# Hybrid retention and attention block on one core: GpSimd's sums for the first projection units, the last gates and the first tokens' keys placed elsewhere

## The reference, cut to what matters

```python
rq, rk, rv, rg, fq, fk, fv, ff = jnp.split(proj, points, axis=-1)
ret = retention(rotary(heads(rq, RET_HEADS), pos),
                rotary(heads(rk, RET_HEADS), pos) * (RET_DK ** -0.5),
                heads(rv, RET_HEADS))[:, PAD:]
ret = head_norm(ret).reshape(b, l, RET_HEADS * RET_DV) * jax.nn.silu(rg)
fox = forgetting_attention(heads(fq, FOX_HEADS), heads(fk, FOX_HEADS), heads(fv, FOX_HEADS), pad(logf))[:, PAD:]
mixed = jnp.concatenate([ret, fox], axis=-1).astype(h.dtype)
```

## Time and profile before

| | |
|---|---|
| three runs | 2966.33, 2971.05, 2980.05 us |
| median | 2971.05 us |
| profiled execution, own time | 2969.91 us |
| its span | 2968.1 us |
| last retention head and pair projection in the span | about 526 to 863 us |

### The profile page before, as it was taken

One profiled execution on the slowest core, in us unless ns is written; L12 is line 12 of the kernel. 1 busy time (PEld: TensorE's weight loads), 2 busy tenths in 40 slices (PEclk: granted clock), 3 DMA queues, 4 the chain that ended last, 5 costly groups with the idle time before them and its releaser, 6 DMA issues.

```text
span 2968.1 us, 40210 instructions
## 1 busy us (share of the span) xinstructions
PE 2885.6 (97%) x14600; PEld 2089.5 (70%) x14600; DVE 1444.0 (49%) x4030; ACT 630.8 (21%) x1285; POOL 1272.9 (43%) x1140
## 2 busy tenths in 40 slices
PE   8999999999999999998999999999999999999998
PEld 4478888888875555554555767787777777777765
DVE  6665656565246767663677532333333333332326
ACT  2222111210025555452111101011111111111114
POOL 3443434366730110101345334555555555555645
PEclk9999999999999999999999999999999999999999
DMA  6500010111120103005444457888898899999996
GB/s 221 177 6 13 18 44 1 29 29 29 31 71 7 55 10 115 12 7 192 150 144 159 128 189 226 249 276 268 262 273 269 267 289 279 307 303 302 316 260 249
DMA packets 181015, 462.08 MB, mean 156 GB/s; under 512 B 26072, under 2 KB 98600, under 8 KB 155080
## 3 DMA queue, kind: packets, MB, share of 16 engines
q1 hardware_dynamic: 133872, 339.23, 32.4%
q0 software_dynamic: 44640, 111.84, 15.9%
q10 hardware_dynamic: 2304, 8.39, 0.7%
HBM read 345.44 MB, written 113.92 MB: 155 GB/s over the span
## 4 chain that ended last, share of the span: by engine, by line
PE 52%; DVE 1%; issue 1%; POOL 0%; ACT 0%
PE ps L2861 24%; PE ps L2802 12%; PE ps L2661 8%; PE ps L2717 3%; PE ps L2799 2%; PE ps L2727 1%; PE ps L2680 1%; PE ps L2750 0%; PE ps L2671 0%; POOL moe_fin L2456 0%; PE ps L2648 0%; PE ps L2701 0%; DVE moe_xT L2018 0%; PE ps L2690 0%; DVE moe_fin L2106 0%
## 5 line engine op out<-in xcount | busy, mean ns | idle before, releaser
L2374 POOL DMA_INDIRECT moe_xg<-t_rows,index x433 | 417.9, 965 | 173.7 <-issue 141.5
L2861 PEld LDWEIGHTS ps<-moe_xT,moe_wg 128*128 128x128 f32 x2048 | 353.0, 196 | 48.1 <-issue 34.3
L2861 PE MATMUL ps<-moe_xT,moe_wg 128*128 128x192 f32 (+22 forms) x2048 | 379.6, 338 | 3.3 <-issue 3.1
L2861 PE MATMUL ps<-moe_xT,moe_wu 128*128 128x192 f32 (+22 forms) x2048 | 376.1, 337 | 0.0
L2861 PEld LDWEIGHTS ps<-moe_xT,moe_wu 128*128 128x128 f32 x2048 | 354.1, 196 | 4.8
L2802 PE MATMUL ps<-moe_wd,moe_hh 128*128 128x512 f32 (+12 forms) x800 | 353.9, 592 | 0.0
L1918 DVE TENSOR_TENSOR moe_hh<-moe_sl,ps 128x256 f32<-128x256 f32 (+19 forms) x144 | 53.6, 372 | 561.8 <-ACT moe_sl L2515 329.6
L2395 POOL DMA_INDIRECT base_rows<-moe_yo,index x100 | 165.0, 1650 | 371.6 <-DVE moe_yo L2032 282.3
L2802 PEld LDWEIGHTS ps<-moe_wd,moe_hh 128*128 128x128 f32 (+12 forms) x800 | 142.3, 180 | 169.1 <-issue 168.8
L2018 DVE STREAM_TRANSPOSE moe_xT<-moe_xg 128x256 f32<-128x256 f32 x433 | 235.3, 609 | 47.2 <-DMA moe_xg<-t_rows,index 41.2
L1253 POOL TENSOR_TENSOR fox_diag<-fox_c,fox_causal 128x128 f32<-128x128 f32 x128 | 55.9, 458 | 449.7 <-DVE fox_mx L1282 444.9
(11 more groups left out here) (352 smaller groups left out, 4652.4 us busy)
## 6 DMA issues: line engine op xcount, KB each, us to landing
moe_wg<-in_we_gate SPq DMA_DIRECT2D x64, 1024.0 KB
moe_wu<-in_we_up SPq DMA_DIRECT2D x64, 1024.0 KB
moe_wd<-in_we_down SPq DMA_DIRECT2D x64, 1024.0 KB
fox_c<-ck SPq DMA_DIRECT2D x8, 1032.0 KB, 8.9
emb_xin<-in_x SPq DMA_DIRECT2D x16, 512.0 KB, 3.9
h_rows<-emb_hr SPq DMA_DIRECT2D x16, 512.0 KB, 2.8
ret_w<-in_w_in SPq DMA_DIRECT2D x16, 512.0 KB, 6.6
moe_yt<-h_rows SPq DMA_DIRECT2D x16, 512.0 KB
```

The source lines that it names most:

```text
L2374: pool.indirect_dma_start(out=xg[g % NXG][:, :], out_offset=None, in_=quarters, in_offset=bass.IndirectOffsetOnAxis(ap=route.index4[:, AT4 ...
L2861: ins = pe.matmul(out, w[:, c, f:FF:FC], xT[u][:, c, 0:n], start=(c == 0), stop=(c == DC - 1))
```

## The change

Three things are moved, and one of them takes fewer matmuls.

*Sums for the first units.* The four token sums of fox unit 0 are no longer made behind the last retention round, but one each in the last head's rounds j = 2 to 5, behind the round's own token sums. Pair 0's weight sums, four in round 5 before, are made in rounds 6 and 7, two each. Unit 1's token sums wait for the first product of the fox projection instead of the last one of the retention.

*Last gates.* The eight gate pairs of the last head stood four each in units 1 and 2, behind the adds of `SIXTH`, `SEVENTH`, `FIFTH` and `FOURTH`. They stand two each in units 1 to 4 now, behind `SEVENTH` and `FOURTH`.

*First tokens' keys.* For pairs 1 to 3 they are multiplied behind unit i = 1 of the pair before, with the key weights not changed yet: eight matmuls. For that TensorE waits for the pair's key weights to have landed, and part 1 of the weight sums waits for the keys. A list `ORDER` counts the products.

```diff
@@ -267,7 +267,6 @@
 
 
 FOX_UNITS = SEQ // BANK
-FOX_PRODUCTS = 1 + PRODUCTS * FOX_UNITS
 
 
 def fox_weight_sums(eng, ahead, p, part):
@@ -280,6 +279,8 @@
         eng.tensor_tensor(s1[:, :, :], wk[:, 0:k, :], wk[:, k:DC, :], ALU.add).then_inc(made, 1)
     if part == 1:
         eng.wait_ge(made, 4 * p + 1)
+        if p >= 1:
+            eng.wait_ge(ahead.fox_proj, ahead.fox_meta_done(p))
         eng.tensor_tensor(wk[:, 0:k, :], wk[:, 0:k, :], wq[:, 0:k, :], ALU.subtract).then_inc(made, 1)
     if part == 2:
         eng.wait_ge(made, 4 * p + 1)
@@ -289,18 +290,22 @@
         eng.tensor_tensor(s4[:, :, :], wq[:, k:DC, :], s2[:, :, :], ALU.subtract).then_inc(made, 1)
 
 
-def fox_token_sums(eng, ahead, hT, g):
+def fox_token_sum(eng, ahead, hT, g, part):
 
     k, s, made = DC // 2, ahead.ftok[g], ahead.fox_tsum
     t0 = META + BANK * (g % FOX_UNITS)
     t1, t2 = t0 + 2 * P, t0 + 4 * P
     b11, b12, b21, b22 = hT[:, 0:k, t0:t1], hT[:, 0:k, t1:t2], hT[:, k:DC, t0:t1], hT[:, k:DC, t1:t2]
-    eng.tensor_tensor(s[:, 0, :, :], b12, b11, ALU.subtract).then_inc(made, 1)
-    eng.tensor_tensor(s[:, 2, :, :], b12, b22, ALU.subtract).then_inc(made, 1)
-    eng.wait_ge(made, 4 * g + 1)
-    eng.tensor_tensor(s[:, 1, :, :], b22, s[:, 0, :, :], ALU.subtract).then_inc(made, 1)
-    eng.wait_ge(made, 4 * g + 3)
-    eng.tensor_tensor(s[:, 3, :, :], b21, s[:, 1, :, :], ALU.subtract).then_inc(made, 1)
+    if part == 0:
+        eng.tensor_tensor(s[:, 0, :, :], b12, b11, ALU.subtract).then_inc(made, 1)
+    if part == 1:
+        eng.tensor_tensor(s[:, 2, :, :], b12, b22, ALU.subtract).then_inc(made, 1)
+    if part == 2:
+        eng.wait_ge(made, 4 * g + 1)
+        eng.tensor_tensor(s[:, 1, :, :], b22, s[:, 0, :, :], ALU.subtract).then_inc(made, 1)
+    if part == 3:
+        eng.wait_ge(made, 4 * g + 3)
+        eng.tensor_tensor(s[:, 3, :, :], b21, s[:, 1, :, :], ALU.subtract).then_inc(made, 1)
 
 
 def flat(ap):
@@ -761,12 +766,14 @@
                 if j in (4, 5) and h + 1 < RH:
                     weight_sums(pool, ahead, h + 1, 2 * (j - 4))
                     weight_sums(pool, ahead, h + 1, 2 * (j - 4) + 1)
-                if j == 5 and h == RH - 1:
-                    for part in range(4):
-                        fox_weight_sums(pool, ahead, 0, part)
-            fox_token_sums(pool, ahead, hT, 0)
-            pool.wait_ge(proj, RH * HEAD_PRODUCTS)
-            fox_token_sums(pool, ahead, hT, 1)
+                if 2 <= j < 6 and h == RH - 1:
+                    fox_token_sum(pool, ahead, hT, 0, j - 2)
+                if j >= 6 and h == RH - 1:
+                    fox_weight_sums(pool, ahead, 0, 2 * j - 12)
+                    fox_weight_sums(pool, ahead, 0, 2 * j - 11)
+            pool.wait_ge(ahead.fox_proj, 1)
+            for part in range(4):
+                fox_token_sum(pool, ahead, hT, 1, part)
             norm(RH - 1)
 
         @block.scalar
@@ -1118,15 +1125,28 @@
         step0 = [sum(steps[:n]) for n in range(NT + 1)]
         FUNITS = [(p, i) for p in range(PAIRS) for i in range(FOX_UNITS)]
 
+        ORDER = []
+        for g, (p, i) in enumerate(FUNITS):
+            ORDER += [(g, which) for which in range(PRODUCTS)]
+            if g == 0:
+                ORDER.append(("meta", 0))
+            if i == 1 and p + 1 < PAIRS:
+                ORDER.append(("meta", p + 1))
+        COUNT = {what: n + 1 for n, what in enumerate(ORDER)}
+
         def done(g, product):
 
-            p, i = FUNITS[g]
-            return FOX_PRODUCTS * p + PRODUCTS * i + (i > 0) + product + 1
+            return COUNT[g, product]
 
         def meta_done(p):
 
-            return FOX_PRODUCTS * p + PRODUCTS + 1
-
+            return COUNT["meta", p]
+
+        def pair_done(p):
+
+            return COUNT[FOX_UNITS * (p + 1) - 1, THIRD]
+
+        ahead.fox_meta_done = meta_done
         ADDS = {SIXTH: 1, SECOND: 2, SEVENTH: 3, FIFTH: 5, FOURTH: 6, THIRD: 7}
         RING = (0, 1, 3, 2, 4, 5, 6, 7)
         groups = [[list(range(s, min(s + 2, z))) for s in range(0, z, 2)] for z in steps]
@@ -1209,20 +1229,20 @@
                 for b in range(2):
                     sp.dma_start(ahead.mix[b][:, :], mixed[P * b:P * (b + 1), :]).then_inc(ahead.mix_in[b], 16)
 
-            sp.wait_ge(proj, FOX_PRODUCTS)
+            sp.wait_ge(proj, pair_done(0))
             sp.wait_ge(ahead.fox_wsum, 4 * 2)
             weights(2)
-            sp.wait_ge(proj, 2 * FOX_PRODUCTS)
+            sp.wait_ge(proj, pair_done(1))
             sp.wait_ge(ahead.fox_wsum, 4 * 3)
             weights(3)
-            sp.wait_ge(proj, 3 * FOX_PRODUCTS)
+            sp.wait_ge(proj, pair_done(2))
             sp.wait_ge(added, PRODUCTS * 3 * FOX_UNITS)
             pair_gates(0)
             sp.wait_ge(proj, done(len(FUNITS) - 2, THIRD))
             sp.dma_start(causal[:, :], square[:, SQ_CAUSAL:SQ_CAUSAL + P]).then_inc(tab, 16)
             pair_values(0)
             pair_values(1)
-            sp.wait_ge(proj, PAIRS * FOX_PRODUCTS)
+            sp.wait_ge(proj, len(ORDER))
             pair_gates(1)
             for n, (p, t) in enumerate(order):
                 if n == 2 * TILES + 1:
@@ -1238,7 +1258,8 @@
             for g in range(2, len(FUNITS)):
                 if g >= 3:
                     pool.wait_ge(proj, done(g - 2, THIRD))
-                fox_token_sums(pool, ahead, hT, g)
+                for part in range(4):
+                    fox_token_sum(pool, ahead, hT, g, part)
             pool.memset(onesf[:, :], 1.0).then_inc(ones_set, 1)
             pool.wait_ge(tab, 16)
             for n, (p, t) in enumerate(order):
@@ -1333,19 +1354,18 @@
                 n0, t0, t1 = PRODUCTS * g, BANK * i, META + BANK * i
                 *p1, u2, u3, u4 = ahead.fadd[p]
                 p1 = p1[g % 2]
-                gate = lambda x: ahead.gate_pair(dve, RH - 1, x + 4 * (g - 1)) if g in (1, 2) else None
+                gate = lambda x: ahead.gate_pair(dve, RH - 1, x + 2 * (g - 1)) if 1 <= g < 5 else None
                 dve.wait_ge(first_c, g + 1)
                 dve.wait_ge(proj, done(g, SIXTH))
                 if g >= 1:
                     dve.wait_ge(added, n0 - PRODUCTS + 5)
                 add(g, SIXTH, u2[:, :], p1[:, :])
-                gate(0)
                 dve.wait_ge(proj, done(g, SECOND))
                 add(g, SECOND, qT[p][:, t0:t0 + 2 * P], p1[:, :])
                 dve.wait_ge(proj, done(g, SEVENTH))
                 dve.wait_ge(added, n0 + 1)
                 add(g, SEVENTH, u3[:, :], u2[:, :])
-                gate(1)
+                gate(0)
                 dve.wait_ge(proj, done(g, FIFTH))
                 if g >= 1:
                     dve.wait_ge(added, n0)
@@ -1354,10 +1374,9 @@
                 if g == 0:
                     dve.wait_ge(*ahead.mix_out[0])
                 add(g, FIFTH, kT[p][:, t1 + 2 * P:t1 + 4 * P], u3[:, :])
-                gate(2)
                 dve.wait_ge(proj, done(g, FOURTH))
                 add(g, FOURTH, kT[p][:, t1:t1 + 2 * P], u3[:, :])
-                gate(3)
+                gate(1)
                 if i >= 2 and p + 1 < PAIRS:
                     for part in (2 * i - 4, 2 * i - 3):
                         fox_weight_sums(dve, ahead, p + 1, part)
@@ -1368,7 +1387,7 @@
             dve.wait_ge(*ahead.ret_att)
             for g in range(len(FUNITS)):
                 project(g)
-            dve.wait_ge(proj, PAIRS * FOX_PRODUCTS)
+            dve.wait_ge(proj, len(ORDER))
             dve.wait_ge(*ahead.mix_out[1])
             for u in range(len(units[0])):
                 bias(0, u)
@@ -1433,9 +1452,9 @@
                 if g >= 2:
                     act.wait_ge(added, PRODUCTS * (g - 2) + 2)
                 nc.scalar.copy(ahead.fadd[p][g % 2][:, :], ps[:, RING[(done(g, FIRST) - 1) % len(RING)], 0:2 * P]).then_inc(first_c, 1)
-                if i == 0:
-                    act.wait_ge(proj, meta_done(p))
-                    nc.scalar.copy(kT[p][:, 0:META], ps[:, RING[(meta_done(p) - 1) % len(RING)], 0:META]).then_inc(meta_c, 1)
+                for m in [x for x in range(PAIRS) if x == 0 == g or x >= 1 and g == FOX_UNITS * (x - 1) + 1]:
+                    act.wait_ge(proj, meta_done(m))
+                    nc.scalar.copy(kT[m][:, 0:META], ps[:, RING[(meta_done(m) - 1) % len(RING)], 0:META]).then_inc(meta_c, 1)
                 if i == 2 and p + 1 < PAIRS:
                     act.wait_ge(w_s[0], 16 * (p + 2))
                     wq = flat(ahead.wqks[p + 1][0][:, :, :])
@@ -1469,16 +1488,13 @@
                     pe.wait_ge(*ahead.v_copied)
                 old = count - len(RING)
                 if old >= 1:
-                    p, x = divmod(old - 1, FOX_PRODUCTS)
-                    if x == PRODUCTS:
-                        pe.wait_ge(meta_c, p + 1)
+                    g, product = ORDER[old - 1]
+                    if g == "meta":
+                        pe.wait_ge(meta_c, product + 1)
+                    elif product == FIRST:
```

(20 more changed lines are left out.)

## The result

| | before | changed |
|---|---|---|
| median, measured side by side | 2966.55 us (2964.69 to 2980.05) | 2954.43 us (2953.49 to 2958.96) |
| profiled execution | 2969.91 us, span 2968.1 | 2953.49 us, span 2951.7 |
| ratio | | 0.995, interval 0.9931 to 0.9968 |

On another chip the same pair stood at 2969.48 and 2959.69 us (0.997, 0.9959 to 0.9981).

A forecast was written before the change was run, and what follows sets the result against it. TensorE, busy for 97% of the span, was taken as the bound. Keys 2.7 + last head 4.2 - gates 0.5 = 6.4 us off 2969.91 gave 2963.5, with 1.1 for the median 2964.6 us; range 2956 to 2974.

The forecast's parts named there:

- Last head: Last retention head's steps: 5.0 us of lost time go, 0.8 comes back behind round j = 2; 4.2 us off.
- Keys: First tokens' keys in pairs 1 to 3: four of twelve matmuls fewer each, 2.7 us off on TensorE's path.
- Gates: Projection units 2 to 4: weight sums still caught by GpSimd, TensorE's stall and slow clock 6.2 for 5.7, 0.5 us lost.
- rival B: Second gate's L665 in unit 3 misses its window: 2.3 us more, 2967, or 2970 if caught singly; chance 0.15.
- Store: Head 3's store delays pair 2's weights in SP's queue; they land at 22, wanted at 24.2: hidden by 2 us.
- Rival E: Norm's small power also blocks the last head's rotations at j = 2: 1.2 us more, 2966; chance 0.08.
- rival C: Rotations pushed over the next round in all six rounds with an extra GpSimd operation: slower, 2976 us; chance 0.07.
- A shift before the attention passes on to the end one for one, since TensorE is the bound behind it as well.: Step of the sum: the whole 6.4 us gained before the attention reaches the end of the execution.
- So such a wait brings no slow clock: In rival A: after 2.28 us of idle in the last head the next turn lasts 0.38 as all do.
- Cost nothing: Later start of unit 1's token sums: they end at 11 and are wanted at 16.5, so no cost.
- Zero cost: Moved keys' new VectorE wait before the in-place difference: covered by six products (10 us), so no cost.
- the half per cent: 15 us, about what a measurement can tell from no change; chances: faster 0.10, slower 0.04, the same 0.86.

The follow-up runs named there:

- the kernel with the one line put back: Kernel before with the moved sums alone, but unit 1's sums again wait for the last retention product; 2966.32 against 2969.93 us for before (0.9989).

## Why the prediction was right, and where it was wrong

In the last head and the projection the mechanism came as described. *Last head*: one rotation caught behind j = 2, one in the next step, TensorE idle for 0.79 us for 0.8 forecast (1.0 on the step); heads 4.1 us shorter where the clock episodes are alike (472.25 and 468.11), for 4.2. *Keys*: sixteen records in pairs 1 to 3, no wait at them. *Gates*: the wait before `SIXTH` of unit 4 is 4.3 us in three of four executions, for 4.4, with the slow clock behind it, by the forecast way, but for L666 in place of L670 being caught in the first gate. In the fourth it is 6.54, 2.2 more, for which rival B had 2.3; the prediction's margins there are 0.1 us, so that the profile of the result fell on the forecast's side is luck in part. *Store*: hidden; once the wait of 4.3 was gone, and with gates caught, so that the last was done 15.0 us behind unit 4's start for the 12 forecast, 1.7 us of it came into view; the cover was about as thin as forecast. Rival E is refuted by the 0.28 beside the power, rival C by even steps.

Wrong was the size, 6.4 us forecast and 12.1 measured. These steps failed:

1. *"A shift before the attention passes on to the end one for one, since TensorE is the bound behind it as well."* It doesn't. With twelve matmuls fewer, one of the two waits for issue in the shared experts goes: 1.8 us net, a term that the prediction put at nothing and that is in none of its rivals.
2. *"So such a wait brings no slow clock"*, read from one turn of 0.38 behind 2.28 us of idle. With the old last head the step behind it lasted 10.5 us in 4 of 7 executions and 8.8 in the others, so removing the wait was worth 5.0 and about half of 1.7 more: an estimate of 0.9 us from these counts.
3. *The unchanged heads were taken as constant.* Their clock episodes differ by up to 3.4 us between executions, and the two profiles of the result had the two ends. This is in the 16.4 us between the profiled executions; in a median it averages out.
4. *The base.* The median of three, 2971.05, was 4.5 above that of six executions beside the changed kernel: 2966.55 less 6.4 is 2960.2. Of the 10.2 us between the forecast 2964.6 and the measured 2954.43 these are 4.5, and the size of the gain is the other 5.7.

Steps 1 and 2 are 2.7 of the 5.7; the cause of the other 3 is open. Where they lie can be said. Over three executions of before and four of the changed kernel, on more than one chip, the heads are 5.6 shorter, the projection 2.7 (forecast 2.2), the shared experts to the end 1.9, and the rest, which no part of the change reaches, 3.9; 14.1 in all. Of the rest, 1.5 us lie between the scores and the output projection (511.0 before, 509.5 changed). Other kernels, with and without each part, show both values and some between, and what sets it is open.

Two more steps were wrong but cost nothing in the whole. The start of unit 1's sums: "Cost nothing" looked only at when TensorE wants the sums; they also push GpSimd into VectorE's gates, 3.6 us with the sums alone. The prediction's walk began at unit 2 and did not see it. In the whole only two gate pairs stand in unit 1, one of them was caught, and VectorE had idle time again before unit 2:

```profile
665.21 2.16 DVE L666 TENSOR_SCALAR ret_ret<-ret_ret,ret_mv,ret_rstd 128x128 f32<-128x128 f32 x2
...
675.34 0.42 DVE L1350 TENSOR_TENSOR fox_u2e<-ps,fox_p10e 128x256 f32<-128x256 f32 x1 [4.87 <-PE ps L1521]
```

The keys: "Zero cost" left out that 1.8 us of keys ahead of unit 2 give VectorE its window back, 4.3 us of gain with the keys alone. The walk through units 2 and 3 of the whole contained these 1.8 us, so its 4.4 us came out right. By the half per cent, "the same" and "faster" are hard to part here: the interval reaches from 3.2 to 6.9 thousandths.

## What to carry to other kernels

Two engines that exclude each other at a port are one resource with two queues: judge a moved operation by whom it meets there, not only by who waits for its result, and put the one that feeds the bound engine first in each free window. Parts of a change that meet in one window must be walked through together; alone, these gave 0.9 and 9.3 us of gain and 7.0 of loss, together 9.8. A wait seen once in a profile has a price with a spread, and so has a stretch that nobody changed; read several executions before taking either as fixed.

## What the runs showed of the hardware

**Waits for issue.** DMA packets of the kind instruction run all through the execution, and each of the 26 waits of TensorE for issue in the shared experts, 0.7 to 4.3 us long, ends 2.2 to 3.7 us after the start of such a packet. That the engine has run through its code there and waits for more is argued from this and not shown. Shown is that 24 records among 14600 more or fewer set whether such a wait stands there once or twice, two thousand microseconds later.

**The clock.** Behind the waits of 2.0 us in heads 1 and 2 TensorE showed 1.2 GHz in 15 of 32 cases and 2.4 in the others, behind the one of 2.3 us in the last head 1.2 in 4 of 7; behind 3.6 us and more that began at 2.4 GHz it was the lower in 35 of 35. In the kernel with the one line put back it also fell without any wait, behind the 24 records of sixteen-column matmuls (L1528), and the next product lasted 3.66 us for 1.89:

```profile
656.81 2.75 PE L1528 MATMUL ps<-hT,fox_w 128*128 128x16 f32 x24
659.40 3.66 PE L1519 MATMUL ps<-hT,fox_w 128*128 128x256 f32 x8
```

Over all 18 executions this came behind 7 of 42 such products of 24 records and behind none of the 30 of 16 records. That may be a further, small gain of the moved keys, but no run isolates it. What decides between the levels behind the short waits was not tried.
